# Recurrence output projection on raw fp32 weights, and the long convolution taken off TensorE

## What is computed

```python
def conv_recurrent_mixer(hn, w_in, conv_a_w, conv_a_b, ln_a_g, ln_a_b,
                         conv_b_w, conv_b_b, w_rg_a, b_rg_a, w_rg_x, b_rg_x, rg_lambda, w_out):
    u = hn @ w_in
    a_val, a_gate, xr, gr = jnp.split(u, [D_A, 2 * D_A, 2 * D_A + D_B], axis=-1)
    ya = a_val * jax.nn.sigmoid(a_gate)
    ya = causal_depthwise_conv(ya, conv_a_w, conv_a_b)
    ya = jax.nn.silu(layer_norm(ya, ln_a_g, ln_a_b))
    xr = causal_depthwise_conv(xr, conv_b_w, conv_b_b)
    yb = rg_lru(xr, w_rg_a, b_rg_a, w_rg_x, b_rg_x, rg_lambda) * jax.nn.gelu(gr)
    return jnp.concatenate([ya, yb], axis=-1) @ w_out
```

## Time and profile before

| | us |
|---|---|
| median of 3 runs | 2341.91 (2341.26 to 2342.76) |
| the profiled execution | 2340.94 |
| its span in the trace | 2339.2 |

### The profile page before, as it was taken

One profiled execution on the slowest core, in us unless ns is written; L12 is line 12 of the kernel. 1 busy time (PEld: TensorE's weight loads), 2 busy tenths in 40 slices (PEclk: granted clock), 3 DMA queues, 4 the chain that ended last, 5 costly groups with the idle time before them and its releaser, 6 DMA issues.

```text
span 2339.2 us, 36867 instructions
## 1 busy us (share of the span) xinstructions
PE 2317.3 (99%) x13004; PEld 2033.0 (87%) x13004; DVE 1513.0 (65%) x1800; ACT 1237.7 (53%) x1552; POOL 76.5 (3%) x71
## 2 busy tenths in 40 slices
PE   8999999999999999999999999999999999999998
PEld 7999998888888888888888888888888888888887
DVE  8899776546546546668776666765555555555676
ACT  7876665445435435456666666555345345345454
POOL 0046100000000000000000000000000000000000
PEclk9999999999999999999999999999999999999999
DMA  8554465655655655655555555566656656656643
GB/s 256 180 181 158 149 209 173 208 174 190 207 177 187 208 180 187 203 179 184 183 180 156 176 171 175 177 192 194 196 181 197 194 181 198 193 181 199 190 152 121
DMA packets 366810, 431.42 MB, mean 184 GB/s; under 512 B 13312, under 2 KB 299136, under 8 KB 366720
## 3 DMA queue, kind: packets, MB, share of 16 engines
q1 hardware_dynamic: 366432, 429.97, 58.0%
q10 hardware_dynamic: 288, 0.23, 0.0%
HBM read 428.05 MB, written 2.10 MB: 184 GB/s over the span
## 4 chain that ended last, share of the span: by engine, by line
PE 93%; DVE 3%; ACT 2%; DMA 1%; issue 0%; SPq 0%; DVEq 0%; ACTq 0%
PE ps L488 32%; PE ps L671 30%; PE ps L494 16%; PE ps L531 3%; PE ps L532 3%; PE ps L533 3%; PE ps L486 2%; PE ps L493 1%; DVE spl L1381 1%; PE O L839 1%; DMA raw<-in_w_in 1%; ACT spl L897 1%; PE O L652 0%; DVE pp L1659 0%; PE Z L626 0%
## 5 line engine op out<-in xcount | busy, mean ns | idle before, releaser
L1381 DVE TENSOR_TENSOR spl<-raw,spl 128x1024 fp32r<-128x1024 f32 x797 | 951.6, 1224 | 580.7 <-ACT spl L897 575.6
L897 ACT ACTIVATE spl<-raw 128x1024 fp32r<-128x1024 f32 (+1 forms) x811 | 832.5, 1055 | 692.2 <-PE ps L671 344.9
L488 PE MATMUL ps<-XA,spl 128*128 128x512 f32 x1792 | 456.0, 393 | 7.8 <-DVE spl L1619 6.7
L488 PE MATMUL ps<-XB,spl 128*128 128x512 f32 x1760 | 462.8, 393 | 0.0
L488 PEld LDWEIGHTS ps<-XA,spl 128*128 128x128 f32 x1792 | 319.2, 189 | 59.0 <-issue 7.2
L671 PE MATMUL ps<-spl,XB 128*128 128x512 f32 x1536 | 349.7, 389 | 0.0
L671 PE MATMUL ps<-spl,XA 128*128 128x512 f32 x1536 | 349.7, 389 | 0.0
L488 PEld LDWEIGHTS ps<-XB,spl 128*128 128x128 f32 x1760 | 305.8, 188 | 42.3
L671 PEld LDWEIGHTS ps<-spl,XB 128*128 128x128 f32 x1536 | 287.8, 188 | 59.5
L671 PEld LDWEIGHTS ps<-spl,XA 128*128 128x128 f32 x1536 | 287.8, 188 | 59.5
L494 PEld LDWEIGHTS ps<-XB,spl 128*128 128x128 f32 x1760 | 259.2, 190 | 31.1
(11 more groups left out here) (214 smaller groups left out, 1790.6 us busy)
## 6 DMA issues: line engine op xcount, KB each, us to landing
raw<-in_w_up SPq DMA_DIRECT2D x256, 512.0 KB, 4.0
raw<-in_w_down SPq DMA_DIRECT2D x256, 512.0 KB, 4.8
raw<-in_w_qkv SPq DMA_DIRECT2D x96, 512.0 KB, 4.6
raw<-in_w_gate SPq DMA_DIRECT2D x64, 512.0 KB, 4.3
raw<-in_w_in SPq DMA_DIRECT2D x63, 512.0 KB, 4.5
raw<-in_w_out SPq DMA_DIRECT2D x32, 512.0 KB, 3.4
raw<-in_w_o SPq DMA_DIRECT2D x32, 512.0 KB, 4.5
raw<-in_w_proj SPq DMA_DIRECT2D x8, 512.0 KB, 4.0
```

The source lines that it names most:

```text
L488: pe.matmul(ps[:, b + o, :], w[:, q, 0, c], x[:, kt, :, :], start=start, stop=False)
L897: return act.activation(out, in_, ACT.Copy, scale=scale)
L1381: dve.tensor_tensor(s[:, :, 1, :], raw[:, m % NRAW, :, :], s[:, :, 0, :].bitcast(F32), ALU.subtract).then_inc(lo_ready, 1)
```

## The change

- The groups 0 to 4 of `G_OUTB` (chunks 66 to 75, `WHOLE`) aren't cut any more. TensorE multiplies the raw fp32 chunk with fp32 `pp` in one fp32 matmul of 256 columns (`whole_weights`, 16 a group) where there were three fp32r matmuls. These chunks need no work of ScalarE, VectorE or GpSimd, and their raw slot is free when TensorE has used it. Groups 5 to 7 stay cut.
- TensorE has no tap of the long convolution any more (54 matmuls and 54 diagonal matrices less). In pair p both tiles have `POOL_TAPS[p]` = 8, 8, 14, 15 taps as ScalarE products (now in 11 slots `prod`) that GpSimd sums, and 23, 23, 17, 16 taps on VectorE. GpSimd adds to the two tiles in turn, so an addition waits for the one before the last.
- GpSimd makes 6 low halves, not 12.
- Much is written in another order: VectorE starts a pair's taps later against the projections, has no low halves to make between chunk 65 and chunk 76, and cuts `yb` (`lo_of(XB, 8, 8, ...)`) after the last `conv_end`. ScalarE makes all 30 products of the last pair before it rounds chunk 76. The first mean stays in the middle of group 4.

The core of the diff:

```diff
-NDG = 22
-TAPS_PE = (14, 14, 14, 12)
-TAPS_POOL = 12
-FIRSTS = CA - TAPS_POOL
-
-
-def taps_upto(pair):
-
-    return sum(TAPS_PE[:pair])
+POOL_TAPS = (8, 8, 14, 15)
+NPROD = 11
...
-SUMMED = tuple(k for k in range(C_GLU + 17, C_PLE0, 2) if (k - C_GLU - 17) % 8 < 6)
+SUMMED = tuple(k for k in range(C_GLU + 17, C_OUTB, 2) if (k - C_GLU - 17) % 8 < 6)
+WHOLE_GROUPS = 5
+WHOLE = range(C_OUTB, C_OUTB + 2 * WHOLE_GROUPS)
...
-            for n, m in enumerate(SUMMED):
-                pool.wait_ge(hi_ready, m + 1)
+            def lo_of_chunk(m):
+
+                pool.wait_ge(hi_ready, halved(m + 1))
                 w = spl[:, m % NSPL, :, :, :]
                 pool.tensor_tensor(w[:, :, 1, :], raw[:, m % NRAW, :, :], w[:, :, 0, :].bitcast(F32),
                                    ALU.subtract).then_inc(lo_summed[m % NSPL], 16)
-                pair, turn = n // 3, n % 3
-                for k in range(max(1, turn * TAPS_POOL // 3), (turn + 1) * TAPS_POOL // 3):
-                    pool.wait_ge(prod_ready, pair * TAPS_POOL + k + 1)
-                    o = y[:, 2 * pair, :]
-                    if k == 1:
-                        pool.tensor_tensor(o, prod[:, prod_slot(pair, 0), :], prod[:, prod_slot(pair, 1), :],
-                                           ALU.add).then_inc(pool_step, 1)
+
+            def add_products(pair, a, b):
+
+                for n in range(max(a, 2), b):
+                    g = products_upto(pair) + n
+                    pool.wait_ge(prod_ready, g + 1)
+                    o = y[:, 2 * pair + n % 2, :]
+                    if n >= 4:
+                        pool.wait_ge(pool_step, added_with(pair, n - 2))
+                        first = o
                     else:
-                        pool.wait_ge(pool_step, pool_adds(pair, k - 1))
-                        pool.tensor_tensor(o, o, prod[:, prod_slot(pair, k), :], ALU.add).then_inc(pool_step, 1)
+                        first = prod[:, (g - 2) % NPROD, :]
+                    pool.tensor_tensor(o, first, prod[:, g % NPROD, :], ALU.add).then_inc(pool_step, 1)
+
+            for pair in range(4):
+                for turn in range(3):
+                    if pair < 2:
+                        lo_of_chunk(SUMMED[3 * pair + turn])
+                    n = 2 * POOL_TAPS[pair]
+                    add_products(pair, turn * n // 3, (turn + 1) * n // 3)
...
+            def whole_weights(g, m, x, mid=None):
+
+
+                pe.wait_ge(sum_ready, g - 3)
+                pe.wait_ge(rg_vec, 12)
+                for j in range(2):
+                    if mid is not None and j == 1:
+                        mid()
+                    pe.wait_ge(raw_landed[(m + j) % NRAW], 16 * ((m + j) // NRAW + 1))
+                    for q in range(4):
+                        for o in range(2):
+                            mm = pe.matmul(ps[:, g % 4, o * 256:(o + 1) * 256], raw[:, (m + j) % NRAW, q, o * P:(o + 1) * P],
+                                           x[:, 4 * j + q, :], start=(j == 0 and q == 0 and o == 0),
+                                           stop=(j == 1 and q == 3), skip_group_check=True)
...
-            for c in range(1, 4):
-                small_gemm(G_GLU + 2 * c, C_GLU + 8 * c, XA, None, rows, None if c == 1 else lambda: conv(c - 2, 2, 3))
-                small_gemm(G_GLU + 2 * c + 1, C_GLU + 8 * c + 4, XA, None, rows, lambda: conv(c - 1, 0, 3))
-                conv(c - 1, 1, 3)
+            for g in range(2, 8):
+                small_gemm(G_GLU + g, C_GLU + 4 * g, XA, None, rows)
...
-            mids = {0: lambda: conv(2, 2, 3), 4: lambda: ln_mean(1)}
-            for s in range(NG):
+            for s in range(WHOLE_GROUPS):
+                whole_weights(G_OUTB + s, C_OUTB + 2 * s, pp, (lambda: ln_mean(1)) if s == 4 else None)
+            for s in range(WHOLE_GROUPS, NG):
                 if s == 6:
                     ln_mean(2)
-                small_gemm(G_OUTB + s, C_OUTB + 2 * s, XB, [(yb_tiles, 1), (yb_tiles, 1)], (8, 12), mids.get(s))
-                if s < 4:
-                    conv(3, s, 4)
+                small_gemm(G_OUTB + s, C_OUTB + 2 * s, XB, [(yb_tiles, 1), (yb_tiles, 1)], (8, 12))
...
+            products(3, 0, 2 * POOL_TAPS[3])
+            m = WHOLE[-1] + 1
+            split(m)
+            act.wait_ge(ln_vec, 1)
+            act.activation(dec[:, :, :], y[:, :, :], ACT.Square).then_inc(ln_act, 1)
+            for q in range(1, 4):
+                split(m + q)
+            act.wait_ge(ln_stat, 2)
+            act.activation(nacc[:, :], Z[:, 0, 0:256], ACT.Sqrt, bias=epsb[:, :]).then_inc(ln_act, 1)
+            for q in range(4, 7):
+                split(m + q)
+            ln_silu(0)
+            split(m + 7)
...
+            def conv(pair, a, b):
+
+
+                p, base = pair % 2 * T, steps_upto(pair)
+                if a == 0:
                     dve.wait_ge(glu_ready, pair + 1)
-                for n in range(q * FIRSTS // 8, (q + 1) * FIRSTS // 8):
-                    x, w = glu[:, 2 * pair, n:n + T], par_col(pair * (2 * CA) + (CONV_A_W + n))
-                    if n == 0:
-                        r = dve.tensor_scalar(first, x, w, par_col(pair * 2 + CONV_A_B), ALU.mult, ALU.add)
+                for n in range(a, b):
+                    t, j, o = 2 * pair + n % 2, n // 2, Z[:, n % 2, p:p + T]
+                    x, w = glu[:, t, j:j + T], par_col(t * CA + (CONV_A_W + j))
+                    if j == 0:
+                        r = dve.tensor_scalar(o, x, w, par_col(t + CONV_A_B), ALU.mult, ALU.add)
                     else:
-                        dve.wait_ge(conv_step, base + n + seconds(n - 1))
-                        r = dve.scalar_tensor_tensor(out=first, in0=x, scalar=w, in1=first, op0=ALU.mult, op1=ALU.add)
+                        dve.wait_ge(conv_step, base + n - 1)
+                        r = dve.scalar_tensor_tensor(out=o, in0=x, scalar=w, in1=o, op0=ALU.mult, op1=ALU.add)
...
+            n1 = 2 * (CA - POOL_TAPS[1])
+            conv(1, 23, 43)
+            glu_value(3)
+            conv(1, 43, n1)
+            conv(2, 0, 14)
+            conv_end(1)
+            conv(2, 14, 18)
+            glu_gate(3, lambda: conv(2, 18, 21))
...
+            conv(2, 21, n2)
+            add_outb(0)
+            conv(3, 0, 14)
+            conv_end(2)
+            add_outb(1)
+            conv(3, 14, 26)
+            add_outb(2)
+            conv(3, 26, n3)
+            conv_end(3)
+            dve.wait_ge(rg_act, 11)
+            lo_of(XB, 8, 8, pp[:, 0:8, :]).then_inc(yb_tiles, 1)
+            add_outb(3)
+            split(m)
+            dve.wait_ge(ln_stat, 1)
+            dve.tensor_tensor(y[:, :, :], y[:, :, :], bcast(Z[:, 0, 0:256], 8), ALU.subtract).then_inc(ln_vec, 1)
+            add_outb(4)
+            split(m + 1)
+            dve.wait_ge(ln_act, 1)
+            tree(nacc[:, :])
+            split(m + 2)
+            split(m + 3)
+            add_outb(5)
```

More of the change, by code:

```diff
@@ L163, in trunk @@
                 nc.sbuf_tensor("rg", [P, 8, 2, T], F32) as rg:
-            prod = rest[:, 0:NPROD * T].rearrange("p (k n) -> p k n", k=NPROD)
+            pass
         XB = sb("XB", [P, NT, 2, T], F32R)
@@ L824, in _ @@
             rg_head(3, 1)
-            def conv(pair, part, parts):
-                if part == 0 and pair == 0:
-                    pe.wait_ge(rg_act, 7)
-                if part == 0:
-                    pe.wait_ge(glu_ready, pair + 1)
-                if part == 0 and pair >= 2:
-                    pe.wait_ge(conv_taken, pair - 1)
-                n = TAPS_PE[pair]
-                for k in range(part * n // parts, (part + 1) * n // parts):
-                    tap = taps_upto(pair) + k
-                    pe.wait_ge(dg_ready, tap + 1)
-                    pe.matmul(O[:, pair % 2, 0:256], dg[:, tap % NDG, :], glu[:, bass.ds(pair * 2 + 1, 1), k:k + T],
-                              start=(k == 0), stop=(k == n - 1), skip_group_check=True).then_inc(dg_used, 1)
             rows = (0, 4, 8, 12)
@@ L1856, in conv @@
                     r.then_inc(conv_step, 1)
-                    if seconds(n + 1) > seconds(n):
-                        j = seconds(n)
-                        x = glu[:, 2 * pair + 1, on_pe + j:on_pe + j + T]
-                        w = par_col(pair * (2 * CA) + (CONV_A_W + CA + on_pe + j))
-                        if j == 0:
-                            r = dve.tensor_scalar(second, x, w, par_col(pair * 2 + (1 + CONV_A_B)), ALU.mult, ALU.add)
-                        else:
-                            n0 = max(k for k in range(n) if seconds(k + 1) > seconds(k))
-                            dve.wait_ge(conv_step, base + n0 + 1 + j)
-                            r = dve.scalar_tensor_tensor(out=second, in0=x, scalar=w, in1=second,
-                                                         op0=ALU.mult, op1=ALU.add)
-                        r.then_inc(conv_step, 1)
@@ L1870, in conv @@
[L1870 to L1885 removed]
+            def conv_end(pair):
```

(31 more changed lines are left out.)

159 lines of the change are left out of this document (55 added, 104 removed).

## The result

The changed kernel takes 2345.03 us (median of 20 runs, 2343.23 to 2347.17), the kernel before, run beside it, 2341.55 us (20 runs, 2340.62 to 2344.41). The ratio is 1.0014, with a 95% interval of 1.0008 to 1.0021: 3.5 us slower by the medians. The interval excludes no change, though the difference is under the 0.2% that the prediction set as its limit. A gain of 7.7 us was forecast. The profiled execution spans 2342.7 us.

The account below looks back on a forecast made before the run. TensorE was taken as barely first, VectorE and GpSimd nearly level at the first mean. Mean from 248.15 to 235.0, 5.4 us given back behind: 7.7 us less, predicted median 2334.2 us, 8-in-10 range 2331.5 to 2342.5.

Parts of the forecast that it names:

- half a us for instructions of either that wait for the other: Before the first mean: allowance for VectorE and GpSimd instructions blocking each other, half a us, giving the mean at 235.0.
- the sum holds: Whole forecast: 248.15 - 235.0 ahead of the mean, 5.4 given back behind it, 7.7 us less, 2334.2.
- The rival on the other side: Pairs 2 and 3: VectorE's taps without a pause slow GpSimd's additions to 1.1 us each; 2349.6 us, chance 0.08.
- GpSimd's step: Time per GpSimd addition in a row of independent ones: bounds 0.70 and 0.88 us, 0.74 taken.
- TensorE's work ahead of the mean: Up to the first mean: fewer taps, dearer products, 18.1 us less work, so TensorE stands at the mean at 228.2.
- pair 2 released: VectorE ahead of the mean: its work up to releasing pair 2 ends at 187.2 us, before at 191.6.
- Pair 3 was released: VectorE ahead of the mean: pair 3 released 22.9 us after pair 2, at 210.1.
- Behind the mean: From the first mean to `G_PLE0`: 26.5 us for 21.1 before, through waits for chunks 77 and 80, giving back 5.4.
- the clock rival: Around the first mean: TensorE's clock falls to half rate in its wait, costing nothing to about 2 us; 2336.2, chance 0.18.
- From `G_PLE0` to the MLP: Behind `G_PLE0` all is as before, so a shift of that point is kept to the end; MLP starting near 319.

Follow-up runs that it names:

- the run with gaps: The changed kernel, but each GpSimd addition waits for the one before it, not the one before that: 2340.37 us, ratio 0.9996 to the kernel before.

## Why the prediction was wrong

**The step that failed** is half a sentence: "half a us for instructions of either that wait for the other". The prediction had the right pair of engines and the right kind of instruction. It priced such a meeting as one wait, for one addition. That price holds in pairs 0 and 1, where the sum that met a row lost 0.36 us. The four sums of pairs 1 and 2 that met the rows of 24 and 26 lost 12.6 us instead. Without that loss the sum holds: with the sums in PSUM the mean is at 234.18 where 235.0 was forecast, and the time 2332.4 where 2334.2 was. The rows to read it from were few before the change. The earlier trace rows show a half of GpSimd at 3.39 for 2.41 and an addition at 2.59 for 0.74, which is GpSimd waiting for VectorE. In the other direction VectorE's longest half in that trace took 1.96 for 1.22 and its longest sum 1.12 for 0.42, so it never waited longer than one instruction of GpSimd. But there each addition waited for the one before, and there were never more than four in a row. The change made rows of 24 and 26 without that wait. The prediction counted how long each row is (20.7 us), and that taps pass it, but not that the instruction behind the taps could meet a row with 4 and 9 us still to go.

**The rival on the other side** had the wrong victim. It took GpSimd's additions to be slowed by VectorE. In the long rows they were not (0.69 a step, at the lower bound); VectorE was stopped by them. That its time, 2349.6, lies nearer to the result than the forecast does is no support for it.

What the Trainium skill says bears on the size. The page cited in the prediction (GPSIMD Engine Reference, Key points) names the contention and the kind of VectorE instruction, and the trace agrees with both. Another page of the Trainium skill (SBUF — State Buffer, Who interferes with whom) says that whichever instruction comes first holds the shared ports for its whole length and the other blocks. Read as a wait for one instruction, that gives, as an estimate from GpSimd's step, at most 0.7 us per sum. The trace agrees in pairs 0 and 1 (0.36 us), and differs in the long rows: the longest sum took 8.8 us, and waited for some twelve additions:

```profile
L1871 DVE TENSOR_TENSOR nacc<-nacc,y x4: 424/2564/8795, 206.3 to 236.4; 128x256 f32<-128x256 f32 x4
```

(the four sums of pairs 1 and 2 in the changed kernel: shortest, median and longest in ns).

**What held**, point by point:
- TensorE's work ahead of the mean: forecast to end at 228.2, ended at 228.9, raw matmuls 0.43 apart.
- GpSimd's step: bounds 0.70 and 0.88, taken 0.74, measured 0.69 in a row of independent additions; the run with gaps gives 0.87 to 0.89, so both bounds were the right two cases. Pair 3 ended at 231.8 once VectorE was free to release it (232.0 forecast, ahead of the sums).
- VectorE's taps 0.39 apart, pair 2 released at 190.1 (187.2 forecast). That is 2.9 late. VectorE's halves and first sum in pairs 0 and 1 lost 4.9 us to GpSimd there, against 1.5 up to that point before the change; one half alone lost 2.16 (3.38 us long, beside a half of GpSimd). The forecast had no term for more such waits. Pair 3 was released at 215.5 (210.1 forecast): 4.3 of these 5.4 are the blocked sum; with the sums in PSUM it is 211.2.
- Behind the mean 26.6 us (26.5 forecast), in the changed kernel and with the sum in PSUM alike. Chunk 77 started 10.4 us after the mean (10.3 forecast). The clock's fall stretched chunk 75, and the wait for chunk 77 was shorter for it, 1.33 and not 3.4: the fall is hidden there, as the clock rival had said.
- The clock fell in the wait, at a price of nothing that showed in the changed kernel.
- From `G_PLE0` to the MLP 57.7 us (57.6 before), and the shift of 4.3 us there is 3.5 in the medians.

**What stays open.** The runs show that the rows of 24 and 26 at 0.69 a step kept the sums out, and that the same rows at 0.87 or 0.89 a step let them in. They don't show what decides it: in the rows of five and six, also without a gap, VectorE's instructions got in. Whether the length of the row matters, the tiles that the engines work on, or something else, was not tried. Nor was it tried how short a gap would do, or how the kernel before would fare with its sums in PSUM; its six sums took 0.42 to 1.12 us each, so there is little to win there.

## What to carry to other kernels

When a change lengthens a row of GpSimd instructions on SBUF, look for every VectorE instruction with two SBUF inputs that will stand beside the row, and give it two prices: one instruction of GpSimd, as in the short rows here, and the rest of the row, as in the long ones. A blocked instruction shows in the profile as a long one (8.8 us for 0.42), not as a wait. Three ways out were measured here: one input in PSUM (12.6 us less by the medians), the instruction behind the row (11.3), or small gaps in it (4.7, since GpSimd then takes 9.4 longer). And a wait that is removed by filling it, or by keeping the clock up, is worth only what the next engine in the chain can follow: read the next wait first.

## What the runs showed of the hardware

- Rows of 24 and 26 GpSimd additions 0.69 us apart kept out a VectorE sum with two SBUF inputs until the row ended; the longest sum took 8.8 us. The sum ended 0.28 us after the row. The same rows with additions 0.87 to 0.89 apart let it in within about one addition (longest sum 0.84 for 0.42).
- In rows of five and six additions, 0.69 to 0.70 us apart and also without a gap, VectorE instructions with two SBUF inputs waited for the running addition only (a half 1.59 for 1.22, a sum 0.78 for 0.42).
- VectorE instructions with one input in SBUF and one in PSUM took the same time beside such a row as alone (two joins 0.75, two sums 0.90).
- 15.7 us of fp32 matmuls held the granted clock at 1.00 where TensorE else waited for 18.0 us; left unfilled, the clock was 0.62 on average in the wait, 0.66 over the next 6.2 us of work, and 1.00 from 253 on. After a wait of 3.25 us ahead of chunk 77 in the run with the filler the granted clock was 0.50 over the next 5.8 us.
